# A ring of four thirds for the expert weights, with a TensorE body for each position of the ring

## The reference, cut to what matters

```
for each expert e, over the tokens routed to it:
    g, lin = split(x @ w_gu[e] + b_gu[e])
    act    = min(g, 7) * sigmoid(1.702 * min(g, 7)) * (clip(lin, -7, 7) + 1)
    y      = act @ w_down[e] + b_down[e]
    out[token] += gate(token, e) * y
```

## Time and profile before

| | |
|---|---|
| median of 3 runs | 2146.21 us (2138.85 to 4163.29) |
| the profiled execution | 2144.11 us, its span on the core 2142.4 us |
| TensorE busy | 1960.0 us, 91% of the span |
| mean clock granted to TensorE | 0.968 of full speed |
| DMA | 527 MB, 246 GB/s over the span |

### The profile page before, as it was taken

How to read it: one execution, slowest core, us unless ns; L and a number is a source line. 1 busy time by engine, 2 the same in 40 slices (tenths; PEclk the granted TensorE clock), 3 DMA queues, 4 the chain that set the end, 5 groups by cost and what they waited for, 6 DMA issues and landing times.

```text
span 2142.4 us, 53085 instructions
## 1 busy us (share of the span) xinstructions
PE 1960.0 (91%) x20253; PEld 803.5 (38%) x20254; DVE 1004.2 (47%) x2276; ACT 355.7 (17%) x729; POOL 508.6 (24%) x536
## 2 busy tenths in 40 slices
PE   3998999978989989999999998999999999999994
PEld 2443444432424323433343342334333343334332
DVE  6427756345434434444444454444443544444434
ACT  3025311221011111111111111111111111011012
POOL 3000022121312322313131322233233322322322
PEclk9998999988989989999999999999999999999997
DMA  9332126322581773959496969879797897999985
GB/s 330 128 118 78 63 95 196 138 109 97 197 340 29 237 300 95 353 177 355 161 352 224 355 251 367 301 266 391 256 387 252 296 357 266 386 385 338 325 305 187
DMA packets 128956, 527.19 MB, mean 246 GB/s; under 512 B 17184, under 2 KB 47920, under 8 KB 79760
## 3 DMA queue, kind: packets, MB, share of 16 engines
q1 hardware_dynamic: 95344, 470.39, 56.6%
q0 software_dynamic: 33568, 56.29, 11.4%
HBM read 494.22 MB, written 32.38 MB: 246 GB/s over the span
## 4 chain that ended last, share of the span: by engine, by line
PE 74%; DMA 14%; DVE 5%; SPq 3%; ACT 2%; issue 1%; POOL 1%; DVEq 0%; POOLq 0%; ACTq 0%
PE psum L1206 39%; PE psum L1226 21%; DMA big<-in_exp_w_down_dram 6%; DMA big<-in_exp_w_gu_dram 6%; PE psum L1115 5%; PE psum L959 5%; PE psum L1052 2%; SPq L466 1%; DMA big<-in_w_in_dram 1%; PE psum L999 1%; DVE big L1453 1%; SPq L447 0%; PE psum L1159 0%; DVE r L1926 0%; DVE gacc L1391 0%
## 5 line engine op out<-in xcount | busy, mean ns | idle before, releaser
L1206 PE MATMUL psum<-big,r 128*32 128x512 f32 x9152 | 1017.5, 602 | 53.8 <-DMA big<-in_exp_w_gu_dram 42.6
L1206 PEld LDWEIGHTS psum<-big,r 128*32 128x32 f32 x9152 | 290.3, 111 | 732.5 <-issue 653.8
L1226 PE MATMUL psum<-big,r 128*32 128x256 f32 x9152 | 518.3, 385 | 27.3 <-DMA big<-in_exp_w_down_dram 16.4
L1226 PEld LDWEIGHTS psum<-big,r 128*32 128x32 f32 x9152 | 294.1, 111 | 230.1 <-DMA big<-in_exp_w_down_dram 26.3
L859 ACT ACTIVATE r<-r,shift 128x128 f32<-128x128 f32 x376 | 154.2, 480 | 998.8 <-PE psum L1206 941.7
L666 POOL DMA_INDIRECT acc_rows<-r,scatter_idx x143 | 230.8, 1614 | 84.9 <-POOL scatter_idx L697 42.9
L655 POOL COPY gather_idx<-r 128x4 int32 (+1 forms) x48 | 8.9, 186 | 1017.5 <-DVE r L1688 1017.5
L1858 DVE TENSOR_TENSOR r<-psum,r 128x256 f32<-128x256 f32 x143 | 60.6, 424 | 377.7 <-PE psum L1206 376.8
L658 POOL DMA_INDIRECT r<-hs_rows,gather_idx x192 | 192.3, 1002 | 85.3 <-issue 45.4
L1818 DVE STREAM_TRANSPOSE r<-r 128x1024 f32<-128x1024 f32 x47 | 97.9, 2084 | 175.8 <-DMA r<-hs_rows,gather_idx 112.6
L959 PE MATMUL psum<-r,big 128*128 128x512 f32 x384 | 167.8, 598 | 2.8 <-DMA big<-in_w_in_dram 2.8
(11 more groups left out here) (284 smaller groups left out, 975.1 us busy)
## 6 DMA issues: line engine op xcount, KB each, us to landing
big<-in_exp_w_gu_dram SPq DMA_DIRECT2D x256, 1024.0 KB, 10.5
big<-in_exp_w_down_dram SPq DMA_DIRECT2D x128, 1024.0 KB, 14.0
big<-in_ada_w_dram SPq DMA_DIRECT2D x12, 2048.0 KB, 12.8
r<-in_x_dram SPq DMA_DIRECT2D x16, 512.0 KB, 12.5
big<-in_w_in_dram SPq DMA_DIRECT2D x4, 2048.0 KB, 20.3
r<-in_exp_b_gu_dram SPq DMA_DIRECT2D x128, 64.0 KB
big<-in_w_out_dram SPq DMA_DIRECT2D x2, 2048.0 KB, 13.3
hs_rows<-r POOLq DMA_DIRECT2D x8, 512.0 KB, 2.9
```

Of the source, the lines that this page charges most:

```text
L1206: last = pe.matmul(psum[32 * j:32 * j + 32, u, :].rearrange("p (a n) -> p a n", a=2), izT[:, k, u * UNIT:(u + 1) * UNIT], rhs[:, :, 256 * ...
L1226: ins_ = pe.matmul(psum[32 * i:32 * i + 32, 4 + u % 2, 0:256], actT[:, u, f, :], down_slab(f)[:, 256 * i:256 * i + 256], start=(f == 0), s ...
```

## The change

- The memory for weights becomes a ring of **four** thirds; the fourth is `r1`, which is not in use during the experts. Place p takes its three thirds from position 3p modulo 4 on, so that the first third of an expert is free as soon as the expert *two* places back has done its down. The waits of SP move accordingly: `freed[2]` of two places back for the first third, `freed[0]` of the place before for the second, `freed[1]` for the third.
- An expert's weights come in 6 loads of 2 MB, with two sets of semaphores by turns.
- The addresses of the thirds are fixed numbers in TensorE's instructions, so TensorE gets a body for each position: an outer loop that runs seven times over four places, each with its own inner loop over that place's items, and three more places written out behind it. An item is now gate and linear and then down of the same item.
- On DVE the reading of the list and the making of addresses and gates move from behind the activation to ahead of the one-hot table.

```diff
-CHUNKS = 12
+CHUNKS = 6
+THIRDS = 4
...
+        def third_of(place, c):
+            return (3 * place + c) % THIRDS
+        def in_third(third, at, size):
+            if third == THIRDS - 1:
+                return r1[:, at:at + size]
+            return big[:, SLOT_OF_PAIR[2 * third + at // 4096], at % 4096:at % 4096 + size]
...
+        def chunk_tile(place, q):
+            tile = in_third(third_of(place, q // 2), (q % 2) * 4096, 4096)
...
+                done_before, done = done, items_until(place - 1)
                 for q in range(CHUNKS):
-                    if q % 4 == 0:
-                        sp_.wait_ge(freed[q // 4], done)
-                    load_chunk(e, q)
-                    if q == 3:
+                    if q == 0 and place >= 2:
+                        sp_.wait_ge(freed[2], done_before)
+                    if q == 2:
+                        sp_.wait_ge(freed[0], done)
+                    if q == 4:
+                        sp_.wait_ge(freed[1], done)
+                    load_chunk(place, e, q)
+                    if q == 1:
...
-            with pe.Fori(0, last_item) as g:
-                down_of(g)
-                begin_item()
-                gate_and_linear_of(g + 1)
-            down_of(last_item)
+            def items_of(at, start, place):
+                with pe.Fori(start, next_item) as g:
+                    begin_item()
+                    gate_and_linear_of(at, g, place)
+                    down_of(at, g)
+            down_of(0, 0)
+            by_units(pe, next_item, 1, lambda: items_of(0, 1, 0))
+            with pe.Fori(0, (NE - 4) // THIRDS) as i:
+                for at in range(1, THIRDS + 1):
+                    begin_place(at)
+                    items_of(at, first_item, i * THIRDS + at)
+            for place in range(NE - 3, NE):
+                begin_place(place)
+                items_of(place, first_item, place)
...
                 block_rows(g + 1)
+                rows_here(g + 4, step)
+                make_idx(g + 2, step)
+                make_gates(g + 2, step)
                 make_onehot(g + 3)
...
                 by_units(dve, units, 1, activate_1)
-                rows_here(g + 4, step)
-                make_idx(g + 2, step)
-                make_gates(g + 2, step)
                 read_list(g + 5)
```

More of the change, by code:

```diff
@@ L348, in build @@
         items_ready = sem("items_ready")
-        w_arrived = [sem(f"w_arrived{q}") for q in range(CHUNKS)]
+        w_arrived = [[sem(f"w_arrived{q}_{turn}") for q in range(CHUNKS)] for turn in range(2)]
         hot_made = sem("hot_made")
@@ L461, in _, with load_chunk @@
                 sp_.dma_start(h_rows[:, t, :], x[t * P:(t + 1) * P, :]).then_inc(xr_in[t], SEMW)
-            def load_chunk(e, q):
-                sp_.dma_start(chunk_tile(q), chunk_source(e, q)).then_inc(w_arrived[q], SEMW)
+            def load_chunk(place, e, q):
+                sp_.dma_start(chunk_tile(place, q), chunk_source(e, q)).then_inc(w_arrived[place % 2][q], SEMW)
             def bias_in_rows(e, place):
@@ L1197, in wait_unit, with gate_and_linear @@
                 pe.wait_ge(sem_, level)
-            def gate_and_linear(u, half, release=None, first=False, between=None):
+            def gate_and_linear(at, u, half, release=None, first=False, between=None):
                 for k in range(4 * half, 4 * half + 4):
-                    if u == 0:
-                        pe.wait_ge(w_arrived[k], SEMW if first else arrived)
-                    rhs = gu_slab(k).rearrange("p (a n) -> p a n", a=2)
+                    if u == 0 and k % 2 == 0:
+                        pe.wait_ge(w_arrived[at % 2][k // 2], SEMW if first else arrived)
+                    rhs = gu_slab(at, k).rearrange("p (a n) -> p a n", a=2)
                     for j in range(4):
@@ L1214, in gate_and_linear, with down @@
                     last.then_inc(gu_made, 1)
-            def down(u):
+            def down(at, u):
                 for f in range(KT):
@@ L1250, in _ @@
             pe.wait_ge(first_made[0], 1)
-            gate_and_linear(0, 0, first=True, between=lambda k: make_places() if k == 0 else None)
+            gate_and_linear(0, 0, 0, first=True, between=lambda k: make_places() if k == 0 else None)
             pe.wait_ge(first_made[1], 1)
-            gate_and_linear(0, 1, first=True, between=lambda k: make_items() if k == 2 else None)
+            gate_and_linear(0, 0, 1, first=True, between=lambda k: make_items() if k == 2 else None)
             pe.wait_ge(items_ready, 1)
-            for i in range(3):
+            for i in range(2):
                 load_word(0, i)
             begin_item()
-            for i in range(3):
+            for i in range(2):
                 load_word(1, i)
+            pe.reg_load(next_item, items_i[0:1, CUM_ITEMS:CUM_ITEMS + 1])
+            load_end(1)
+            pe.reg_mov(arrived, SEMW)
             for half in range(2):
```

108 lines of the change are left out of this document (56 added, 52 removed).

## The result

The changed kernel takes 2192.49 us (median of 4 runs, 2189.91 to 2193.89), the kernel before 2144.37 beside it: a ratio of 1.0232, 95% interval [1.0206, 1.0257]. It is **slower**, where 2087 us and "faster" was predicted. The profiled run took 2189.91 us.

The account below looks back on a forecast made before the run. TensorE was taken as the bound nearly everywhere, with waits set by when loads may start. Profiled 2144.1 - 78.9 (late weights) + 5 (DVE's order) + 17 (code) = 2087 us; range 2060 to 2125.

Parts of the forecast that it names:

- The fourth third: Weight ring: each third released one phase earlier; of 83.9 us of late weights 5 us stay, a gain of 78.9.
- periods of 42.0, 31.7, 21.4 us: TensorE's times for items of four, three and two units without a wait, expected at all places but 14.
- place 14: The place where one wait for weights stays, its down third landing late; with a rest elsewhere 5 us, between 0 and 12.
- The replay with 3.0 us a piece: Ring followed third by third at 3.0 us for 1 MB, 12 us a third, to find the waits left.
- 2 MB loads: Expert weight loads: no faster transfer booked; one longer piece to wait for, 2.5 to 3.0 us, within the 5 us left.
- DVE's order: Small operations moved ahead of the activation: it can begin 3.0 us later, 5 us in total, between 1 and 8.
- one-unit items: Two items where DVE's later activation is not covered by matmuls; expected at about 19 us each.
- the code term: 17 us in the sum for TensorE fetching its code at returns; by the trace alone it could be 0.
- TensorE's program: Four bodies taken not to stay: six outer-loop returns fetch code at 2.9 us each, 17 us, 0 to 63.
- the six places: Starts of places 5, 9, ... 25: TensorE idle of 2 to 4 us, with some 140 packets of code overall.
- slower by code: Rival: 66 jumps over left-out units each wait 2.9 us, 191 us, giving 2278; decided from 0.9 us a jump; chance 0.07.
- packets at first sight cost no wait: Evidence against the code rival: no TensorE idle when code is first fetched.

Follow-up runs that it names:

- e9: The changed kernel with TensorE's items written out one after another, no loop and no jump over a left-out unit, right for this input only: 2072.75 us.
- e4: The changed kernel with 12 loads of 1 MB an expert in place of 6 of 2 MB: 2194.39 us.
- e6: The changed kernel, unchanged, timed again beside other runs: 2192.17 us, 1.021 of the kernel before.
- e3: The kernel before with DVE's new order alone: 2153.84 us, 0.9726 of the kernel before, which took 2215.7 on this chip.
- e7: The changed kernel without the outer loop, 31 places written out, inner loops and jumps over left-out units kept: 2155.64 us, 1.0045 of the kernel before.
- e13: The straight-line changed kernel plus one jump over 64 never-executed instructions in each of 46 items: 2072.81 us.
- e17: The straight-line changed kernel plus one jump over 256 never-executed instructions in each of 46 items: 2105.88 us.
- e15: The straight-line changed kernel plus one jump over 576 never-executed instructions in each of 46 items: 2308.7 us.
- e5: The kernel before, unchanged, run once for a profile on a chip where it was at 2145: 2148.11 us.
- e18: A one-body version with a parity buffer for the first third of w_gu, 1 MB loads and DVE's old order: 2126.94 us, 0.992 of the kernel before.
- e16: The straight-line changed kernel, DVE's new order, with POOL's gather waiting for the start of down: 2071.92 us, where the kernel before took 2144.3.

## Why the prediction was wrong

- **The fourth third** (83.9 us late, 5 left) was right. In e9 all items but three have the periods of 42.0, 31.7, 21.4 us that I had measured; place 14, the one place named, loses 6.75 us for the 5 predicted, waiting 0.92 and 3.95 us for weights. The replay with 3.0 us a piece held.
- **2 MB loads** booked at nothing: right (e4, 2194.39 for 2192.17 of e6).
- **DVE's order** (5 us): right where the stall is absent. The one-unit items of e9 take 18.4 and 19.5 us (about 19 said) for 17.25 and 17.4, and the first item 65.7 for 65.0: 3.9 together. What I missed is its other side. The order moves the gather away from down, and on a chip with the stall e3 took 62 us less than the kernel before; no row of the profile that I had shows that stall.
- Without the code term my sum was 2070. The changed kernel without jumps and returns, e9, took 2072.75.
- **TensorE's program** (17 us) is the step that failed. It measured 2192.5 - 2072.75 = 119.7 us, across jobs: 36.5 for the returns (e6 less e7) and 83 for the jumps (e7 less e9, where the inner loops go too, which cost next to nothing). I had the six places and nearly the number of packets (163 for 140), but took 2.9 us a return, a small transfer's time, where it is 6.1: TensorE stands 3 to 6 us, though the packet itself takes 1 us, and runs at a lower clock after. What fills the rest of that wait stays open.
- The jumps I had as a rival of 0.07, "slower by code", with a deciding point of 0.9 us a jump. 83 / 66 = 1.26 us: its mechanism is what happened, at less than half its price of 2.9, since most jumps cost nothing and the long ones 3 to 6. My argument against it was that "the jumps are short, a quarter to a half of a packet of code for each unit left out". The mistake was to look at one unit. At the end of down, two left-out units are 256 instructions and three 384, and the same item has skipped as much again by then. e13 to e17 show that up to 192 there is next to no price, at 256 16 jumps of 46 wait, and at 576 all do. In e7 all 13 skips of 256 or 384 at the end of down wait, more than e17's 16 of 46; that the earlier skips of the same item make the difference is argued, no run varies them alone. (The places with a body are 31 and not 30; nothing hangs on it.)
- The evidence "packets at first sight cost no wait" came from code that was run in order, and held only for that: e9 fetches 161 packets and waits for none.

The Trainium skill (Runtime: NRT & Kernel Launch, Instruction fetch mechanics) says that a taken branch out of what is held stops the engine until a fetch is done, and gives it as one reason why kernels prefer full unrolling. The runs agree with both: only e9, with loops and skips written out, is free of the wait, while e7, with the outer loop alone written out, kept 83 us of jumps. In the profile such time has no releaser: a growing "issue", beside more packets on the code's queue and branch instructions of several microseconds, is how it is seen.

## What to carry to other kernels

Before a loop body is multiplied, add up its instructions: one body of about 70 or 86 KB in a loop was not fetched again turn by turn, turns of about 140 and 280 KB were fetched anew every time (the sizes are estimates from the counts of instructions). Once code streams, order is all: in these runs straight code was free, skips of up to 192 instructions cost at most 0.1 us each, and a return or a skip of 576 cost 5 to 8 us. Price a branch by the instructions that it skips, probably together with the other skips just ahead of it, and test such a change once with all its branches written out, for that separates the code's cost from what the change was for.

## What was not expected of the hardware

- A packet of code takes about 1 us, but the jump over 576 instructions (e15) takes 3.3 to 7.3 us. TensorE, which still has matmuls queued, stands for 0.8 to 4.9 of them, and with the lower clock after it a jump costs 5.1 us.
- With DVE's old order, every item of three or four units was some 2.3 us longer on one chip and 3 on another, and none in the other profiles of such kernels (the kernel before, e5, e18); the kernel before had 2192.7 and 2215.7 us where such items appeared, and 2144 to 2145 elsewhere. It was profiled only where it was at 2148 and below; that its own extra time (48 and 71 us) is the same stall is argued, and it is less than the 76 to 78 and 103 to 104 us that the stall takes from the items of the other kernels on these chips. e16 was meant to try the gather under down with the new order, but ran on a chip without the stall.
